# Small attention blocks two at a time in the groups with a projection, and other places for pieces at the first and last groups and the borders

## The reference

```python
# layer 0: 4 heads of differential attention (A), 8 heads of forgetting attention (B), side by side
s = einsum('bqhmd,bkhmd->bmhqk', q, k) * DK_A ** -0.5          # two maps m
p = softmax(where(visible, s + bias, NEG_INF)); w = p[:, 0] - lam * p[:, 1]
oa = rmsnorm(einsum('bhqk,bkhd->bqhd', w, v), subln_g) * (1.0 - lam_init)
logf = log_sigmoid(fz + b_f); cum = cumsum(logf)               # B: s + cum_q - cum_k, causal
# layer 1: 16 heads, own chunk of 64 and 8 chunks before (C), learned relative bias
# every layer
x = x + rmsnorm(mixer(rmsnorm(x, g_pre_mix)) @ w_out, g_post_mix)
u = relu(rmsnorm(x, g_pre_ffn) @ w_up); x = x + rmsnorm((u * u) @ w_down, g_post_ffn)
```

## Time and profile before

| | us |
|---|---|
| median of 3 runs | 2861.58 |
| lowest and highest | 2860.78, 2863.74 |
| profiled execution, its own time | 2858.94 |
| its span, first to last instruction | 2857.1 |
| TensorE, products | 2796.9 (98%) |
| VectorE | 1449.9 (51%) |
| ScalarE | 896.0 (31%) |
| GpSimd | 573.5 (20%) |

### The profile page before, as it was taken

The page is one execution under the profiler, slowest core; times in us unless marked ns, Lnnn a source line. Parts: engine busy times, 40 slices in busy tenths (PEclk is TensorE's granted clock), DMA queues, the critical chain, the costliest instruction groups (busy, mean ns, idle before and its releaser), DMA issues.

```text
span 2857.1 us, 49677 instructions
## 1 busy us (share of the span) xinstructions
PE 2796.9 (98%) x18736; PEld 2681.7 (94%) x18736; DVE 1449.9 (51%) x3470; ACT 896.0 (31%) x1673; POOL 573.5 (20%) x379
## 2 busy tenths in 40 slices
PE   7999999999999999999999999999999999999997
PEld 7899888899999999999989888888999999999997
DVE  6777666657333333333486666665653333333334
ACT  5444433554111111111454333435521111111113
POOL 0111000362212121212320000005512121222124
PEclk9999999999999999999999999999999999999999
DMA  5311111342101010101141111123411111111113
GB/s 184 124 71 58 71 71 70 138 159 78 60 31 59 29 59 29 59 29 59 60 173 61 60 60 60 69 86 123 166 71 38 52 37 51 37 51 37 51 37 126
DMA packets 59005, 210.32 MB, mean 74 GB/s; under 512 B 7000, under 2 KB 16608, under 8 KB 55696
## 3 DMA queue, kind: packets, MB, share of 16 engines
q1 hardware_dynamic: 55504, 174.64, 17.1%
q0 software_dynamic: 3408, 34.42, 3.0%
HBM read 163.36 MB, written 51.97 MB: 75 GB/s over the span
## 4 chain that ended last, share of the span: by engine, by line
PE 91%; DVE 3%; issue 2%; ACT 2%; POOL 1%; DMA 0%; DVEq 0%; ACTq 0%; SPq 0%; POOLq 0%
PE ps L1421 76%; PE ps L1534 4%; PE ps L1552 4%; PE ps L1497 2%; PE ps L1548 1%; PE ps L1507 1%; PE ps L1509 1%; DVE ACC L1032 1%; PE ps L1408 1%; POOL XL L650 0%; PE ps L1401 0%; DVE WL L1075 0%; PE ps L1519 0%; ACT XH L734 0%; DVE XL L1041 0%
## 5 line engine op out<-in xcount | busy, mean ns | idle before, releaser
L1421 PE MATMUL ps<-XH,WH 128*128 128x384 f32 (+1 forms) x3096 | 1025.9, 331 | 15.8 <-DVE WL L1075 11.7
L1421 PE MATMUL ps<-XL,WH 128*128 128x384 f32 (+1 forms) x3096 | 1029.8, 333 | 0.0
L1421 PE MATMUL ps<-XH,WL 128*128 128x384 f32 (+1 forms) x3096 | 1019.9, 329 | 0.0
L1421 PE MATMUL ps<-U,WH 128*128 128x384 f32 (+1 forms) x3072 | 754.1, 329 | 0.0
L568 POOL TENSOR_TENSOR WL<-WS,WH 128x1024 fp32r<-128x1024 f32 x160 | 384.1, 2402 | 1770.2 <-ACT WH L705 1770.2
L1421 PEld LDWEIGHTS ps<-XH,WH 128*128 128x128 f32 x3096 | 583.7, 189 | 28.1 <-issue 22.1
L1421 PEld LDWEIGHTS ps<-XL,WH 128*128 128x128 f32 x3096 | 583.9, 189 | 11.8 <-issue 11.8
L1421 PEld LDWEIGHTS ps<-XH,WL 128*128 128x128 f32 x3096 | 583.9, 189 | 5.1 <-issue 5.1
L1421 PEld LDWEIGHTS ps<-U,WH 128*128 128x128 f32 x3072 | 544.4, 188 | 0.0
L1421 PE MATMUL ps<-U,WL 128*128 128x384 f32 (+1 forms) x1536 | 505.3, 329 | 0.0
L705 ACT CAST WH<-WS 128x1024 fp32r<-128x1024 f32 x209 | 217.7, 1044 | 663.5 <-PE ps L1421 648.5
(11 more groups left out here) (130 smaller groups left out, 2189.5 us busy)
## 6 DMA issues: line engine op xcount, KB each, us to landing
WS<-w_in SPq DMA_DIRECT2D x209, 512.0 KB, 4.5
k_out<-KT SPq DMA_DIRECT2D x16, 672.0 KB, 3.4
x_scr<-XRES POOLq DMA_DIRECT2D x6, 1536.0 KB, 5.4
v_out<-VT SPq DMA_DIRECT2D x16, 544.0 KB, 4.9
o_scr<-OT SPq DMA_DIRECT2D x14, 544.0 KB, 2.7
XRES<-x_scr POOLq DMA_DIRECT2D x4, 1536.0 KB, 8.7
BIAS<-nc_scr SPq DMA_DIRECT2D x8, 672.0 KB, 4.9
toep_scr<-rel_scr SPq DMA_DIRECT2D x1, 5120.0 KB, 23.2
```

The source lines that it names most:

```text
L1421: return pe.matmul(bank[:, 0:w], wt, xt, start=m == 0, stop=m == 3 * tiles - 1, skip_group_check=False)
```

## The change

Three things.

**Slots.** `SLOTS` gives the blocks of each slot of a group with a projection: blocks 3 and 2 share a slot, and 1 and the sample block share one, so seven slots hold the nine blocks and `SLOT_END` has nine ends instead of eleven. The second block of a pair uses the upper 512 columns of PR, the second bank of each map and the upper half of PT; small tiles (M, NM, L, RI, stats, ON) are twice as wide. The last group of a layer keeps one block a slot in the order before. ScalarE's WH for the next group moves from slots 5 and 7 to 4 and 5, Qh, Kh and the low parts from 8 and 9 to 6 and 7.

**First and last groups.** The first group of each layer is a section of its own, out of the loop. Ql and Kl are made before the last V eviction; TensorE waits for that eviction ahead of its first scores. The scans go from ahead of the loop over slots to the end of `sums` of slot 0, and the store of NC has a semaphore of its own (fnc). In the last groups VectorE, not GpSimd, subtracts the first three XL pieces, between its V copy and `sums` of slot 0.

**Borders.** Other ticks: after OUT, chunk 1's ST and `pow` from 7.3 to 6.9 and 7.0, DG from 7.35 to 7.2, its broadcast from 8.25 to 8.5, chunk 2's statistics and broadcast from 10.75 and 11.5 to 11.25 and 12. After FF, chunk 0's DG from 7.5 to 6.94, its broadcast from 9.75 to 9.5, `pre_hi1` of chunk 1 from 7.9 to 8.1, the statistics, power, diagonal and broadcast of chunk 1 about three steps earlier and of chunk 2 about one, and another order on VectorE.

```diff
-ORDER = [7, 6, 5, 4, 3, 2, 1, SAMPLE, 0]
-
-ORDER_LAST = [2, 1, 0, 5, 4, 3, 7, 6, SAMPLE]
-
-
-SLOT_END = {"A": [26, 52, 76, 96, 114, 130, 144, 158, 174, 194, 216],
-            "B": [26, 52, 76, 96, 114, 130, 144, 158, 174, 194, 216],
-            "C": [24, 46, 64, 82, 100, 118, 136, 154, 172, 194, 216],
+
+SLOTS = [[7], [6], [5], [4], [3, 2], [1, SAMPLE], [0]]
+
+SLOTS_LAST = [[2], [1], [0], [5], [4], [3], [7], [6], [SAMPLE]]
+
+
+SLOT_END = {"A": [28, 56, 82, 106, 132, 156, 174, 194, 216],
+            "B": [28, 56, 82, 106, 132, 156, 174, 194, 216],
+            "C": [26, 50, 72, 94, 122, 150, 170, 192, 216],
...
-        self.pace, self.order = (att, ORDER) if proj else ("last", ORDER_LAST)
+        self.pace, self.slots = (att, SLOTS) if proj else ("last", SLOTS_LAST)
+        self.order = [b for slot in self.slots for b in slot]
+
+    def until(self, s):
+
+        return sum(len(slot) for slot in self.slots[:max(s, 0)])
+
+    def blocks(self, s):
+
+        return range(self.until(s), self.until(s + 1)) if 0 <= s < len(self.slots) else ()
+
+    def spot(self, k):
+
+        return next((s, k - self.until(s)) for s in range(len(self.slots)) if k in self.blocks(s))
...
-            attention(0, "A", 0, 4, True)
+            attention(0, "A", 0, 1, True)
+            attention(0, "A", 1, 3, True)
             attention(0, "B", 4, 3, True)
             attention(0, "B", 7, 1, False)
         else:
-            attention(1, "C", 8, 7, True)
+            attention(1, "C", 8, 1, True)
+            attention(1, "C", 9, 6, True)
...
-                pre_sq1=(-4.3, 4.2, 8.9), pre_dg=(-0.3, 7.35, 11.2), pre_rb=(0.8, 8.5, 11.8)),
+                pre_sq1=(-4.3, 4.2, 8.9), pre_dg=(-0.3, 7.2, 11.2), pre_rb=(0.8, 8.5, 11.8)),
     "dve": dict(post_st=(-7.6, 0.9, 5.05), post_x0=(-6.75, 2.0, 6.4), post_x1=(-5.75, 2.75, 7.4), pre_lo0=(-4.75, 3.75, 8.4),
-                pre_lo1=(-4.7, 4.95, 8.5), pre_red0=(-3.6, 6.05, 9.2), pre_red1=(-3.25, 6.1, 9.25), pre_st=(-0.4, 7.3, 10.9)),
-    "pe": dict(post_stat=(-7.75, 0.75, 5.5), post_bc=(-7, 1.75, 6.9), pre_stat=(-0.5, 7.5, 10.75), pre_bc=(0.5, 8.25, 11.5)),
-    "pool": dict(post_pow=(-7.5, 1, 4.95), post_store=(-4.9, 3.6, 8), pre_pow=(-0.4, 7.3, 10.9)),
+                pre_lo1=(-4.7, 4.95, 8.5), pre_red0=(-3.6, 6.05, 9.2), pre_red1=(-3.25, 6.1, 9.25), pre_st=(-0.4, 6.9, 10.9)),
+    "pe": dict(post_stat=(-7.75, 0.75, 5.5), post_bc=(-7, 1.75, 6.9), pre_stat=(-0.5, 7.5, 11.25), pre_bc=(0.5, 8.5, 12)),
+    "pool": dict(post_pow=(-7.5, 1, 4.95), post_store=(-4.9, 3.6, 8), pre_pow=(-0.4, 7.0, 10.9)),
 }
 
 AFTER_FF = {
-    "act": dict(post_dg=(1.9, 5.9, 10.9), pre_hi0=(2.5, 6.9, 12.5), pre_sq0=(2.9, 6.95, 12.9), pre_hi1=(3.5, 7.9, 13.5),
-                pre_sq1=(3.9, 8.5, 13.9), pre_dg=(7.5, 15.5, 16.3), pre_rb=(9.9, 16.1, 16.95)),
+    "act": dict(post_dg=(1.9, 5.9, 10.9), pre_hi0=(2.5, 6.9, 12.5), pre_sq0=(2.9, 6.95, 12.9), pre_hi1=(3.5, 8.1, 13.5),
+                pre_sq1=(3.9, 8.5, 13.9), pre_dg=(6.94, 12.6, 15.5), pre_rb=(9.9, 13.6, 16.1)),
     "dve": dict(post_st=(0.9, 5.1), post_x0=(2.5, 6.9), post_x1=(3.5, 7.9), pre_lo0=(4.5, 8.5), pre_lo1=(4.6, 8.6),
                 pre_red0=(6.2,), pre_red1=(6.25,), pre_st=(7.5,)),
-    "pe": dict(post_stat=(0.75, 6, 10.25), post_bc=(2, 7.25, 11.25), pre_stat=(7.75, 14.6, 15.6), pre_bc=(9.75, 15.75, 16.4)),
-    "pool": dict(post_load=(0, 4, 8), post_pow=(0.95, 4.9, 8.9), post_store=(3.95, 8.5, 14), pre_pow=(6.9, 15.5, 16.5)),
+    "pe": dict(post_stat=(0.75, 6, 10.25), post_bc=(2, 7.25, 11.25), pre_stat=(7.75, 11.75, 14.6), pre_bc=(9.5, 13.25, 15.75)),
+    "pool": dict(post_load=(0, 4, 8), post_pow=(0.95, 4.9, 8.9), post_store=(3.95, 8.5, 14), pre_pow=(6.9, 12, 15)),
...
                         if sec.att == "B":
-                            sp.wait_ge(sem["fst"], 48)
+                            sp.wait_ge(sem["fnc"], 16)
...
-                                for o in range(7):
+                                if c == 0:
+
+                                    pool.wait_ge(sem["olo"], sec.at(i, "olo", 3))
+                                for o in range(0 if c else 3, 7):
...
-                                act.wait_ge(sem["fst"], 48)
-                            for dst, src in turned(kind, sec.order[k], 0):
+                                act.wait_ge(sem["fscan"], 2)
+                                act.wait_ge(sem["fst"], 32)
...
                             if sec.proj:
-                                if s in (5, 7):
-                                    u = (s - 5) // 2
+                                if s in (4, 5):
+                                    u = s - 4
                                     hi_unit(sec, i, u, u, 1, sec.at(i, "D", 3 * u + 3))
-                                if s == 8:
+                                if s == 6:
 
                                     act.wait_ge(sem["S"], sec.at(i, "S", 18))
                                     act.wait_ge(sem["evD"], sec.at(i, "evD", 3))
                                     act.copy(Qh[:, 0:TOK], QT[:, :]).then_inc(sem["qkhi"], 1)
-                                if s == 9:
+                                if s == 7:
...
                     pieces(2, "post_st")
                     empty_next(0, 1)
+                    pieces(1, "pre_red0 pre_red1")
                     pieces(2, "post_x0")
+                    pieces(1, "pre_st")
                     empty_next(2)
-                    pieces(2, "post_x1 pre_lo0 pre_lo1")
-                    pieces(1, "pre_red0 pre_red1 pre_st")
-                    pieces(2, "pre_red0 pre_red1 pre_st")
-                    empty_next(3, 4, 5, 6, 7)
+                    pieces(2, "post_x1 pre_lo0 pre_lo1 pre_red0 pre_red1")
+                    empty_next(3)
+                    pieces(2, "pre_st")
+                    empty_next(4, 5, 6, 7)
...
+                        low_queries(sec.base.get("qkhi", 0) + 1)
+                        low_keys(sec.base.get("qkhi", 0) + 2)
 
                         dve.wait_ge(sem["D"], sec.base["D"])
                         empty_qkv(2, 2, ps[:, 2 if sec.layer else 5, :])
-                        low_queries(sec.base.get("qkhi", 0) + 1)
-                        low_keys(sec.base.get("qkhi", 0) + 2)
                         if sec.layer:
                             low_weights(sec.loaded - 3, 0)
                         low_weights(sec.loaded - 2, 1)
                         low_weights(sec.loaded - 1, 2)
...
+                        for s in range(len(sec.slots) + 2):
+                            if s < len(sec.slots):
+
+                                wait(dve, "T", sec.at(i, "T", 1 + sec.until(s - 1) if s >= 2 else 0))
+                            for k in sec.blocks(s):
+                                scores(k, 0)
+                                scores(k, 1)
                             if s == 0:
                                 dve.wait_ge(sem["T"], sec.at(i, "T", 1))
                                 dve.tensor_copy(V[:, 4:8, :].rearrange("p t q -> p (t q)"), ps[:, 7, :]).then_inc(sem["tD"], 1)
-                            if s >= 2:
-                                empty_output(s - 2)
-                            if 1 <= s <= 9 and kind != "A":
-                                empty_turned(s - 1)
-                            if s < 9:
-                                sums(s)
+                                for o in () if sec.proj else range(3):
+                                    dve.wait_ge(sem["ohi"], sec.at(i, "ohi", o + 1))
+                                    dve.tensor_tensor(ct(XL, 0, o), ct(XL, 0, o).bitcast(f32), ct(XH, 0, o).bitcast(f32), ALU.subtract)\
+                                        .then_inc(sem["olo"], 1)
+                            for k in sec.blocks(s - 2):
+                                empty_output(k)
+                            if kind != "A":
+                                for k in sec.blocks(s - 1):
+                                    empty_turned(k)
+                            for k in sec.blocks(s):
+                                sums(k)
+                            if sec.g0 == 0 and s == 0:
+
+                                dve.wait_ge(sem["flogf"], 2)
+                                dve.wait_ge(sem["zz"], 1)
+                                for t0, t1 in ((0, N_PROMPT), (N_PROMPT, KCOLS)):
+                                    dve.tensor_tensor_scan(NC[:, t0:t1], ZZ[:, t0:t1], LF[:, t0:t1], 0.0, ALU.add, ALU.subtract)\
+                                        .then_inc(sem["fscan"], 1)
...
-                            if sec.proj and s == 8:
+                            if kind == "A":
+                                for k in sec.blocks(s - 2):
+                                    normed(k)
+                            if sec.proj and s == 6:
                                 low_unit(0)
                                 low_queries(sec.at(i, "qkhi", 3))
-                            if sec.proj and s == 9:
```

(60 more changed lines are left out.)

184 lines of the change are left out of this document (89 added, 95 removed).

## The result

The changed kernel takes 2842.59 us (median of 4 runs, 2840.51 to 2843.11), the one before 2861.47 on the same chip: ratio 0.9932, interval 0.992 to 0.9944, faster by 18.9 us. The forecast was 2847. The same program up to 60 us reaches that place up to 1.4 us apart in the traces; this offset is taken off where a single place is compared. Medians also hold what differs from run to run: mostly where short stretches at the lower clock fall. The kernel before had medians of 2861.47, 2861.12, 2860.39 and 2860.37 in the four sets of runs, so a difference of 1 us between medians of different sets shows little.

A forecast was written before the change was run, and what follows sets the result against it. TensorE was taken as the bound, busy 2796.9 of 2857.1 us, its products unchanged. The terms sum to -14.8: profiled 2858.94 to 2844.1, plus 2.6 for the median, 2846.8, said as 2847; own range 2840 to 2853.

The forecast's parts named there:

- going over, A / B / C: TensorE changes between kinds of product less often, two slots fewer per projection group: -2.4 / -2.7 / -6.3, together -11.4 us.
- new wait in C: Tile 3's eviction moves into double slot 4, so TensorE waits 1.5 us before tile 5 in 7 groups: +10.5 us.
- end of an A group: Block pair [1, SAMPLE] has VectorE do one more output ahead of Kl: +0.1 each, +0.4 us.
- first group of layer 0: Ql and Kl start earlier and the scans come later, so the first turning comes at 81.2, not 83.11: -2.4 us.
- attention to MLP, two: At both borders ST, power and DG come earlier and TensorE's waits shrink: -3.4 each, -6.8 us.
- MLP to layer 1, its first scores: Ql and Kl no longer behind V's eviction shorten the first-scores wait; projection chunk 1 no earlier: -2.0 us.
- last groups, two: VectorE does three XL subtractions, then scales undisturbed by GpSimd; first turning 0.8 us earlier each: -1.6 us.
- clock: Four stretches at 1.2 GHz after waits in first or last groups partly go as waits shrink: -1.5 us.
- The four distances of the earlier trace: Extra gaps between TensorE's kinds of product per slot, 0.08, 0.10, 0.08 and 0.10, together 0.36 us.
- the 0.09 that I added by guess: Added per slot for the outputs' last step, whose half-width form must end first: 0.45 us a slot in B and C.
- Double slots keep up: VectorE finishes double slots before TensorE's turnings, with 0.5 us in hand in B, 1 in C, 1.6 in A: no cost.
- the slower rival: VectorE is late in double slots, TensorE waits 28 times; at 1 us each +13, 2875 us; chance 0.05.

The follow-up runs named there:

- experiment 2: Changed kernel with the C groups alone back to one block a slot and the eleven old ends; 2837.46 us, ratio 0.9919.
- Experiment 1: Changed kernel with slot 3 of a C group ending at product 96 instead of 94; 2830.24 us, ratio 0.9895.
- experiment 4: c96 with the scores of a pair's second block six products later in C groups, 14 more visits to the scores; 2837.4 us, ratio 0.9919.
- Experiment 7: Changed kernel, two single undoings: Ql and Kl behind the last V eviction, 2845.12 us; the two scans ahead of the loop over slots, 2846.02 us.
- experiment 6: Changed kernel with the old ticks after FF and VectorE's old order of pieces at the MLP's border into layer 1; 2843.27 us, ratio 0.994.
- experiment 5: Changed kernel with the old ticks after OUT; 2848.39 us, ratio 0.9957.
- experiment 8: c96 with the first groups' low weights of units 1 and 2 behind the sums of slots 1 and 2; 2828.4 us, ratio 0.9888.
- c96: The changed kernel with the edit of Experiment 1, slot 3 of C ending at product 96; 2830.24 us.
- experiment 3: Changed kernel with one block a slot and the old ends in all groups, A, B and C; 2843.89 us, ratio 0.9941.
- experiment 9: Kernel of experiment 8 with the scans behind the scores' eviction of slot 1 instead of behind slot 0's sums; 2828.59 us, ratio 0.9886.

## Why the prediction was right

The forecast was 4 us too slow, with the mechanisms as told and their sizes partly off. Its sum missed the profiled executions by less, -14.8 for -16.6; the rest is that the profiled execution of before lay 2.6 below its median and that of the changed kernel at it. By its own terms (in us; "profile" is from the group periods and from before and after at the same product):

| term | forecast | profile |
|---|---|---|
| going over, A / B / C | -2.4 / -2.7 / -6.3 | -4.0 / -3.7 / -8.2 |
| new wait in C | +10.5 | +11.1 |
| end of an A group | +0.4 | +1.1 |
| first group of layer 0 | -2.4 | -3.3, of it -1.7 clock |
| attention to MLP, two | -6.8 | -6.9 |
| MLP to layer 1, its first scores | -2.0 | -0.6, with +1.7 clock |
| last groups, two | -1.6 | -1.0 and -1.4, of the second -1.7 clock |
| clock | -1.5 | in the rows above |
| sum | -14.8 | -16.9 (measured 16.6) |

Part of the near hit is luck: going over came out at -15.9 for -11.4, outside its bound of 14, and the wait in C, the A groups and the border into layer 1 together took 2.7 us of that back.

- **Going over.** Its price in C is 0.585 a slot (experiment 2 against 1), not 0.45. The four distances of the earlier trace rows were read rightly; the 0.09 that I added by guess is nearer 0.2. B went from 67.8 to 66.5, 0.62 a slot. A's periods fell by 0.36 a slot, for 0.3, but they hold the grown wait for ON, 0.28 us in each of four groups where 0.1 was forecast; without it a slot in A saved 0.50. That A would save less than B and C is thus hardly so. That turning costs nothing was right (experiment 4).
- **The wait in C** came in the place named, seven times, 1.48 us at the product against 1.5; by periods 1.59. Experiment 1 shows its cause. The two errors in C nearly cancel: a C group was to go to 63.0 and went to 62.8.
- **Double slots keep up.** No wait of a turning for M or PR in slots 4 and 5; the slower rival did not come.
- **First group of layer 0.** The first turning came at 80.37, forecast 81.2. The waits shrank by 1.8 us and the clock's stretch went. Experiment 7 adds what the forecast did not see: undoing Ql and Kl early or the scans late alone costs 2.2 and 2.7 us in this group, since each brings a wait and a low stretch.
- **Attention to MLP** was the safest step: DG's wait of 2.53 us is gone entirely, where 0.4 was to stay, and by the traces the borders gained 3.5 and 3.4 us for 3.4 each.
- **MLP to layer 1 is the step that failed.** "I find TensorE at chunk 1 of the projection no earlier (0 to 0.5 later)" had the sign and not the size: its first product stands at 1444.63 for 1457.37, 1.75 us later than the work ahead of it. The wait for GpSimd's sums grew to 1.72 (1.03 before, 1.02 in experiment 6) and a low stretch followed. The wait at the first scores shrank by 1.15 us, for 2.0. The ticks and the order there are worth 1.3 us by the trace (experiment 6).
- **Clock.** The net is as forecast: five lengths of 3.4 us before, four after. But it was booked as a term by itself; it belongs to each border, and there it decides between -0.6 and -2. One of the forecast's own signs of being wrong, the lower clock still in four stretches, is there, one of the four in a new place.

## What to carry to other kernels

Count how often TensorE goes over to the 64-row scores, not only how many products it has: a visit costs 0.5 us here (experiment 4), and putting two blocks into one visit saves this. When slots are merged, look at every buffer that is released at a slot's end: a tile whose last product slips two places over a border is released a whole slot later, and now a double one. Where the bank's next user stands in that same slot, move the border to the tile's end (96, not 94); A's and B's ends do not lie on tile ends either, and no such wait shows there. And price a wait at a section's border with the low stretch that may follow it: of like waits some cost their length and some 1.7 us more.

## What the runs showed of the hardware

- The low stretches last 3.4 or 6.8 us (0.83 and 0.66 in a 10 us window) and come at or behind waits at the borders: one of 1.4 to 3.8 us, or in the last groups several of 0.4 to 1.6 close together. But not behind all: behind 1.45 us at 80.37 none, behind 1.41 at 1480.28 one; behind DG's wait of 2.53 in the kernel before none, behind 2.57 in experiment 5 one; behind 2.19 at the first scores of layer 1 one in experiment 8 and none in c96. The last group of layer 0, the same in both, has one at 520 in the changed kernel and none in c96. What decides it stays open; the sums of experiments 2, 3 and 5 miss by 1 to 2 us through it.
- Taking a wait away on TensorE's first place often uncovers the next on the same engine chain: experiments 7 to 9 moved 1.0 to 2.9 us between the V copy, the turning and slot 2's scores, and taking waits away (8 and 9) brought 0.4 us in layer 0.
